# First two items of every feed-forward stage: W_high against both halves of h in one product of 512 columns

## What is computed

```python
def _swiglu(x, w_gate, w_up, w_down):          # D_MODEL 1024, D_FF 2816
    return (jax.nn.silu(x @ w_gate) * (x @ w_up)) @ w_down

f = _swiglu(_rmsnorm(x, ffn1_pre_g[l]), ffn1_w_gate[l], ffn1_w_up[l], ffn1_w_down[l])
x = x + 0.5 * _rmsnorm(f, ffn1_post_g[l])
...
h = rms_norm(x, ffn_norm[layer])
x = x + swiglu(h, ffn_w_gate[layer], ffn_w_up[layer], ffn_w_down[layer])
```

## Time and profile before

| what | value |
|---|---|
| median of 3 executions | 1088.68 us (1088.61 to 1088.86) |
| span of the profiled execution, first to last instruction | 1087.8 us |
| profiled execution's own time | not given apart; the three executions lie 0.8 to 1.1 us above its span |
| TensorE busy | 1070.8 us, 98% of the span, 7134 products |
| VectorE busy | 791.0 us, 73% |
| ScalarE busy | 588.3 us, 54% |
| GpSimd busy | 218.4 us, 20% |
| mean granted TensorE clock | 0.998 of full speed |
| weights and inputs read | 187.90 MB, 174 GB/s over the span |

### The profile page before, as it was taken

The page is one execution under the profiler, slowest core; times in us unless marked ns, Lnnn a source line. Parts: engine busy times, 40 slices in busy tenths (PEclk is TensorE's granted clock), DMA queues, the critical chain, the costliest instruction groups (busy, mean ns, idle before and its releaser), DMA issues.

```text
span 1087.8 us, 18962 instructions
## 1 busy us (share of the span) xinstructions
PE 1070.8 (98%) x7134; PEld 946.9 (87%) x7134; DVE 791.0 (73%) x1082; ACT 588.3 (54%) x842; POOL 218.4 (20%) x224
## 2 busy tenths in 40 slices
PE   9999999999999999999999999999999999999996
PEld 8888889898788888898998988888899888888886
DVE  5867776887678888766775788877558557776674
ACT  6546544667666545455785644554443565544452
POOL 0006000031069997000000498000000000000001
PEclk9999999999999999999999999999999999999999
DMA  7775455342345656453334655654434235545541
GB/s 256 286 246 205 180 177 207 108 167 78 119 158 192 232 182 231 174 194 116 128 145 155 227 189 198 224 185 175 172 123 162 98 125 186 219 174 190 204 146 40
DMA packets 36514, 189.65 MB, mean 174 GB/s; under 512 B 3824, under 2 KB 4592, under 8 KB 21616
## 3 DMA queue, kind: packets, MB, share of 16 engines
q1 hardware_dynamic: 34016, 181.22, 46.1%
q10 hardware_dynamic: 2160, 6.70, 1.8%
q0 software_dynamic: 288, 1.05, 0.3%
HBM read 187.90 MB, written 1.05 MB: 174 GB/s over the span
## 4 chain that ended last, share of the span: by engine, by line
PE 88%; DVE 6%; ACT 3%; issue 1%; DMA 1%; POOL 0%; POOLq 0%; SPq 0%; ACTq 0%; DVEq 0%
PE ps L529 23%; PE ps L587 20%; PE ps L534 12%; PE ps L620 10%; PE ps L722 6%; PE ps L541 6%; PE ps L561 2%; PE ps L642 1%; DVE gu_low L1668 1%; PE ps L490 1%; PE ps L675 1%; PE ps L706 1%; PE ps L688 1%; ACT gu_high L1083 1%; PE ps L974 1%
## 5 line engine op out<-in xcount | busy, mean ns | idle before, releaser
L529 PE MATMUL ps<-hT,gu_high 128*128 128x512 f32 x1152 | 286.8, 391 | 0.0
L529 PEld LDWEIGHTS ps<-hT,gu_high 128*128 128x128 f32 x1152 | 211.5, 188 | 41.6 <-issue 0.4
L1791 DVE TENSOR_TENSOR gu_low<-gu_raw,gu_high 128x2048 fp32r<-128x2048 f32 x83 | 196.3, 2365 | 7.7 <-ACT gu_high L1189 4.6
L534 PEld LDWEIGHTS ps<-hT,gu_low 128*128 128x128 f32 x1152 | 157.2, 190 | 11.2
L1189 ACT ACTIVATE gu_high<-gu_raw 128x2048 fp32r<-128x2048 f32 x84 | 160.4, 1910 | 9.3 <-PE ps L541 8.2
L534 PE MATMUL ps<-hT,gu_low 128*128 128x256 f32 x1152 | 160.6, 282 | 0.0
L1165 ACT ACTIVATE ffn_s<-ffn_s 128x256 f32<-128x256 f32 x88 | 36.9, 420 | 181.4 <-DVE ffn_s L1758 145.2
L1795 DVE TENSOR_TENSOR dn_low<-dn_raw,dn_high 128x1024 fp32r<-128x1024 f32 x84 | 112.2, 1336 | 2.7 <-ACT dn_high L1197 2.7
L1773 DVE TENSOR_TENSOR ffn_s<-ps,ffn_s 128x256 f32<-128x256 f32 x72 | 30.6, 425 | 108.6 <-ACT ffn_s L1177 108.6
L1668 DVE TENSOR_TENSOR gu_low<-gu_raw,gu_high 128x2048 fp32r<-128x2048 f32 x36 | 83.4, 2317 | 34.6 <-ACT gu_high L1083 34.6
L1197 ACT ACTIVATE dn_high<-dn_raw 128x1024 fp32r<-128x1024 f32 x84 | 88.8, 1057 | 35.6 <-PE ps L587 35.6
(11 more groups left out here) (319 smaller groups left out, 1855.8 us busy)
## 6 DMA issues: line engine op xcount, KB each, us to landing
gu_raw<-in_wgu SPq DMA_DIRECT2D x126, 1024.0 KB, 4.8
dn_raw<-in_wdn SPq DMA_DIRECT2D x88, 512.0 KB, 5.3
x<-in_x SPq DMA_DIRECT2D x2, 512.0 KB, 5.7
gu_raw<-in_wgu SPq DMA_DIRECT2D x2, 512.0 KB, 7.1
scratch<-in_glu ACTq DMA_DIRECT2D x1, 1024.0 KB, 7.5
scratch<-in_biasM ACTq DMA_DIRECT2D x1, 1024.0 KB, 5.0
s5in<-in_s5in ACTq DMA_DIRECT2D x1, 768.0 KB, 4.3
out_x<-scratch SPq DMA_DIRECT2D x3, 256.0 KB, 2.4
```

Source lines behind the costliest of these rows:

```text
L529: nc.tensor.matmul(out, gu[0][:, sl, o:o + P], hT_both[:, k, :, :].rearrange("p a s -> p (a s)"), start=k == 0, stop=False)
L534: i = nc.tensor.matmul(out[:, 0:SEQ], gu[1][:, sl, o:o + P], hT[0][:, k, :], start=False, stop=k == KC - 1)
L1791: nc.vector.tensor_tensor(gu[1][:, sl, :], gu_raw[:, sl, :], gu[0][:, sl, :], ALU.subtract).then_inc(s["gu_split"], 1)
```

## The change

`BOTH` now holds items 0 to 19 of each stage. `gate_up_first` and the `gate_up` of item 1 take the merged form; ScalarE and VectorE get the copies and additions of the two halves for items 0 and 1 too, ScalarE reading item 0's halves from banks 0 and 2. Items 20 and 21 stay as they were. In the changed kernel line 529 is 531, 534 is 536, 561 becomes 562 and 565, 1165 is 1168, 1171 is 1177, 1177 is 1184, 1189 is 1196, 1197 is 1204, and on VectorE lines from 1711 on are 7 higher.

```diff
--- before.py
+++ after.py
@@ -81,7 +81,7 @@
 ORDER1 = (0, 1, 4, 6, 5, 7, 2, 3, 8, 9)
 ORDER2 = (0, 1, 2, 4, 6, 3, 5, 7)
 HEADS = 4
-BOTH = (((2, 20),),) * 4
+BOTH = (((0, 20),),) * 4
 
 
 def both_at(f, i):
@@ -523,6 +523,8 @@
                     if first == 0 and w == 1:
                         pe.wait_ge(s["gu_split"], item + 1)
                     out = bank(4 + 2 * w + h)
+                    if both and between is not None and w == 1:
+                        between()
                     if both:
                         for k in range(KC):
                             o = (w * KC + k) * P
@@ -557,10 +559,11 @@
                     wait_hT(n, k)
                     for w in range(2):
                         o = (w * KC + k) * P
-                        for pw_, px in PASSES:
-                            i = nc.tensor.matmul(bank(2 * w)[:, 0:SEQ], gu[pw_][:, sl, o:o + P], hT[px][:, k, :],
-                                                 start=(pw_, px, k) == (0, 0, 0),
-                                                 stop=(pw_, px, k) == (1, 0, KC - 1))
+                        nc.tensor.matmul(bank(2 * w), gu[0][:, sl, o:o + P],
+                                         hT_both[:, k, :, :].rearrange("p a s -> p (a s)"),
+                                         start=k == 0, stop=False)
+                        i = nc.tensor.matmul(bank(2 * w)[:, 0:SEQ], gu[1][:, sl, o:o + P], hT[0][:, k, :],
+                                             start=False, stop=k == KC - 1)
                         if k == KC - 1:
                             i.then_inc(s["gate_ready" if w == 0 else "up_ready"], 1)
 
@@ -592,10 +595,10 @@
             def ffn(f, n, after_two=None):
                 base, G0 = FFN_ITEM[f], FCH * f
                 gate_up_first(base % 2, base, G0, n, after_two)
-                gate_up(1, 1 - base % 2, base + 1, G0 + 1, first=n,
+                gate_up(1, 1 - base % 2, base + 1, G0 + 1, both_at(f, 1), first=n,
                         between=lambda: broadcast_rinv((0, None, 1, None, 3, None, 5)[n], 1))
                 down(0, G0, start=True)
-                edges = sorted({2, FCH, *(e for pair in BOTH[f] for e in pair)})
+                edges = sorted({2, FCH, *(e for pair in BOTH[f] for e in pair if e > 2)})
                 for first, end in zip(edges, edges[1:]):
                     with pe.Fori(first // 2, end // 2) as r:
                         for h in range(2):
@@ -1165,16 +1168,20 @@
                         nc.scalar.activation(sil_s[:, h, :], sil_s[:, h, :], ACT.Silu) \
                           .then_inc(s["silu_ready"], 1)
 
+                    gate, up = (bank(0), bank(2)) if static and i == 0 else (bank(4 + h), bank(6 + h))
+                    reused = not static or G0 + i >= 2
                     if both:
                         act.wait_ge(s["gate_ready"], plain(G0 + 1))
-                        act.wait_ge(s["prod_done"], plain(G0 - 1))
-                        nc.scalar.activation(sil_s[:, h, :], bank(4 + h)[:, SEQ:], ACT.Copy).then_inc(s["gate_rest"], 1)
+                        if reused:
+                            act.wait_ge(s["prod_done"], plain(G0 - 1))
+                        nc.scalar.activation(sil_s[:, h, :], gate[:, SEQ:], ACT.Copy).then_inc(s["gate_rest"], 1)
                     if not late:
                         silu()
                     if both:
                         act.wait_ge(s["up_ready"], plain(G0 + 1))
-                        act.wait_ge(s["act_ready"], plain(G0 - 1))
-                        nc.scalar.activation(prod_s[:, h, :], bank(6 + h)[:, SEQ:], ACT.Copy).then_inc(s["up_rest"], 1)
+                        if reused:
+                            act.wait_ge(s["act_ready"], plain(G0 - 1))
+                        nc.scalar.activation(prod_s[:, h, :], up[:, SEQ:], ACT.Copy).then_inc(s["up_rest"], 1)
                     if static and i == FCH - 1 and f < 2:
                         act.wait_ge(gu_loaded[sl], arrived(base + 2))
                         act.wait_ge(s["gate_ready"], plain(G0 + 1))
```

## The result

The changed kernel takes 1093.92 us (median of 5 executions, 1093.58 to 1094.15) against 1088.86 us (1088.61 to 1089.17, 5 executions) of the kernel before on the same chip: ratio 1.0047, 95% interval 1.0036 to 1.0057. It is slower by 5.06 us. The forecast was 1092.2 us, range 1089.9 to 1094.4: sign and range held, and the loss was put 1.5 us too small.

The account below looks back on a forecast made before the run. TensorE was taken to bound the kernel, with each opening ending on VectorE's chain. Stage losses of 1.45 + 1.25 + 0.58 + 0.24 = 3.5 us, saving included, took the median from 1088.68 to 1092.2 us, range 1089.9 to 1094.4.

Parts of the forecast that it names:

- What bounds the kernel: Whole span: TensorE, busy 98%; a change counts only if TensorE does less or is made to wait.
- Part 1: TensorE's gate and up products of items 0 and 1: 0.015 us saved a block, 1.9 us over 128 blocks.
- Part 2: Opening of stage 1: TensorE's saving is waited away, and the longer chain makes `down(0)` 1.45 us later.
- Part 3: Openings of stages 2 to 4: chain grows by one addition, less 0.22 head start, +0.24 us at each `down(0)`.
- Part 4: Behind item 1: VectorE 1.40 us late, carrying over 1.0 us in stage 2 and 0.34 in stage 3.
- I take the undisturbed value: VectorE's carry-over in stages 2 and 3 (1.0 and 0.34) priced nearest the rows, though it may vanish or double.
- the sign: What would show the forecast right: VectorE 1.0 to 1.3 us later at item 2 of stages 2 and 3.
- the tightest of stage 3: `down` of item 7: `act_low` ended 0.57 us ahead, 0.42 more than a release takes, leaving +0.58 in all.
- A: At `down(0)`: the additions stay hidden and only TensorE's 1.9 us saving shows, 1086.8 us; chance 0.05.
- B: Only `down(0)` of each stage is late, nothing is carried on: +2.2 us, 1090.9 us; chance 0.20.
- D: Scaling and product of items 0 and 1, stages 2 and 3: GpSimd stretches them, 1094.0 us; chance 0.15.
- E: Stage 1's longer idle time: TensorE's clock falls, adding 2.8 us, 1095.0 us; chance 0.05.

Follow-up runs that it names:

- Bare products: TensorE as in the changed kernel, ScalarE and VectorE as before, the halves of items 0 and 1 never added: 1088.51 us, ratio 0.9998.
- the bare chain: Changed kernel's copies and additions for items 0 and 1, first half copied times zero, with TensorE's three passes as before: 1093.92 us, ratio 1.0042.
- item-0: Changed kernel with only item 0 of each stage merged, item 1 keeping its three passes: 1091.44 us, ratio 1.002.
- item-1: Changed kernel with only item 1 of each stage merged, `gate_up_first` back to three passes: 1090.69 us, ratio 1.0016.
- the hold: GpSimd's table work of stages 2 and 3 held back until item 4's activation: changed kernel 1089.24 us, kernel before 1086.73 us.

## Why the prediction was right in sign and too small

**What bounds the kernel**, and that each opening ends with VectorE's chain: right. Bare products gained nothing, the bare chain lost everything.

**Part 1, 0.015 us a block.** Not confirmed for `gate_up_first`. The 512-column product of one block, of the next and of the tenth after the first, in the opening of stage 1 of the changed kernel:

```profile
12.33 0.40 PE L562 MATMUL ps<-hT,gu_high 128*128 128x512 f32 x1
...
12.68 0.40 PE L562 MATMUL ps<-hT,gu_high 128*128 128x512 f32 x1
...
15.86 0.40 PE L562 MATMUL ps<-hT,gu_high 128*128 128x512 f32 x1
```

Ten blocks take 15.86 - 12.33 = 3.53, 0.353 each and not 0.345: alternating the two products gives back half of the saving. The choice "same price, since three-pass products alternate too" was wrong. It changed little, because the saving was waited away. The 0.0025 us a block that I worked out from the Trainium skill, "TensorE: Matmul & The Clock Gate", section "Wait — 56ns, not 53.3ns?", lies below the 0.007 that the alternating order measured, and the trace decides for 0.007.

**Part 2, stage 1, +1.45 at `down(0)`.** It measured 1.58 from the broadcast, and 1.47 at the stage's end (the idle time 1.74 for 1.9). Right, but for 0.1 us that later items do give back. The item-0 and item-1 runs put all of it on item 0.

**Part 3, +0.24 at each of three `down(0)`.** From the last `down` of the stage before, it came 0.16, 0.58 and 0.42 later. With the hold the three are 0.27, 0.28 and 0.25, so the working was right for an undisturbed opening, and the 0.24 a little small: at 0.007 a block for 0.015 (part 1), the 0.10 of head start from `gate_up_first` becomes 0.06, and 0.24 becomes 0.28. The 0.58 of stage 3 is GpSimd beside item 0: product, cast and `act_low` took 0.62, 0.37 and 0.49, together 0.33 more than the 0.43, 0.29 and 0.43 of an undisturbed item. VectorE's timeline of the changed kernel:

```profile
615.71 0.62 DVE L1783 TENSOR_TENSOR ffn_s<-ffn_s 128x256 f32<-128x256 f32 x1 [0.22 <-ACT ffn_s L1168]
616.36 0.37 DVE L1788 CAST act_high<-ffn_s 128x256 fp32r<-128x256 f32 x1
616.76 0.49 DVE L1790 TENSOR_TENSOR act_low<-ffn_s,act_high 128x256 fp32r<-128x256 f32 x1
...
625.12 2.82 DVE L1798 TENSOR_TENSOR gu_low<-gu_raw,gu_high 128x2048 fp32r<-128x2048 f32 x1
```

In stage 4, 0.14 of the 0.42 lies ahead of its first product, in the mixer between, and that is no more than the mixer differs from one profile to the next (see the table). The opening itself grew by 0.28.

**Part 4, what VectorE carries on: the step that failed.** I had 1.01 behind `down(0)` in stage 2 and 0.34 in stage 3. They measured 169.56 - 168.11 = 1.45 and 167.49 - 166.60 = 0.89; with what stage 3 lost at `down(0)` above its 0.24, this is nearly all of the 1.5 us that the forecast fell short. The sizing of this term failed at "I take the undisturbed value": the prediction itself had said that the carry-over may vanish or double, since GpSimd's instructions would meet other ones, and it came nearly to double. In stage 2 the working holds up to item 1: `gu_low` of that step starts at 330.37, after 328.25 before, 2.12, of which 0.99 is what stage 1 had lost, so 1.13 late for 1.25. Then `dn_low`, stretched from 1.22 to 2.06, makes VectorE 1.97 late at item 2 (334.56 for 331.60), where 1.0 to 1.3 had been named as the sign. VectorE was to be 1.0 late behind item 1 of stage 3; `gu_low` of that step came at 625.12 instead of 620.43, 4.69, of which 2.60 is what the stages before had lost: 2.09 late. Nor was the place right: the `down` of item 7 was taken as the tightest of stage 3, and most of the loss behind `down(0)` came at items 3 to 5, where the kernel before has no wait at all. The runs with the hold say more: the lateness of the chain would not have come through at all, because VectorE has 2.75 us to spare at item 3. It comes through only since GpSimd eats that spare time, and with VectorE later, more of what TensorE waits for was stretched. I had the right ingredients with the wrong mechanism between them: not a lateness handed on, but new meetings that the lateness brings about. That the range still held the result is in part luck, since nothing in the prediction worked out how VectorE and GpSimd would meet.

**The rivals.** A fell (down(0) moved). B, nothing carried on, is what the kernel does with the hold and not without it. D named the mechanism that was missing, and its 1094.0 is the nearest number; but its price was put on the two forms that the change exposes, scaling and product of items 0 and 1 in stages 2 and 3. Of these eight three stretched, to 0.45, 0.56 and 0.62 for 0.42, about 0.4 us in all where the rival had 2.4 before slack; its own sign, above 0.6, was met once (615.71). The large losses are instructions that read two SBUF tensors in either kernel: `act_low` 2.57, `dn_low` 2.06, the scaling of item 3 2.18. So D's number was near by luck. The rule from the Trainium skill, "GPSIMD Engine Reference", section "1. Specifications", that GpSimd contends with VectorE instructions with two SBUF inputs, agrees with the traces: `act_low` took up to 2.57 us with GpSimd at work and never over 0.43 without. E fell: the granted clock in the stretch with the 1.74 us of idle time stayed at 1.00.

```profile
23.00:26.00 3.00, 1.26 (x7) 1.00 0.03 5
```

## What to carry to other kernels

A cheaper form of a product that leaves a sum to another engine pays only where that engine's chain has more slack than the sum costs: read first whether the wait behind the product is already ended by that engine. Where a third engine slows the second, do not price lateness by undisturbed durations, and try holding the third engine's work back until the stage runs evenly; that one wait was worth more here (2.3 us of the kernel before) than the change could ever have been (1.9 us at most by part 1). And give the start of a long chain, here the broadcast, its place ahead of the work that can hide it.

## What the runs showed of the hardware

While GpSimd worked, VectorE's instructions with two SBUF inputs took up to six times as long (`act_low`, 256 columns: 424 ns least, 2569 most) and also the cast with one input (295 ns median, 809 most), whereas the same addition with an operand in PSUM never moved. The durations (least, median, most) of the changed kernel's lines 1788, 1790 and 1780:

```profile
L1788 DVE CAST act_high<-ffn_s x88: 293/295/809, 24.0 to 1078.9; 128x256 fp32r<-128x256 f32 x88
```

```profile
L1790 DVE TENSOR_TENSOR act_low<-ffn_s,act_high x88: 424/426/2569, 24.3 to 1079.3; 128x256 fp32r<-128x256 f32 x88
```

```profile
L1780 DVE TENSOR_TENSOR ffn_s<-ps,ffn_s x80: 417/425/426, 23.1 to 1062.0; 128x256 f32<-128x256 f32 x80
```

That is not luck in when they ran. Of the 80 additions of line 1780, 24 lay for more than half of their time beside a GpSimd instruction, and none took more than 426 ns. Of the 88 `act_low`, 23 did, with a median of 664 ns, while the 65 with no GpSimd instruction beside them took 427 at most. The size is not fixed: a product with two SBUF inputs took its usual 0.42 us within GpSimd's 4.49 us instruction (337.12), the scaling before it 0.80. Two products of 512 and 256 columns in turn cost 0.353 us a pair, eight of one and then eight of the other 0.345; I had not expected a price for the order, and did not test what makes it.
